# Attention of a hybrid decoder step: probabilities turned two iterations after their scores, with three probability buffers

## What is computed

```python
x = x + 0.5 * swiglu(x, norm_ffn1_g, w_ffn1_in, w_ffn1_out)
q, k, v, qi, ki, wi, lx, lg, qm, gates = mix_inputs(x)        # rmsnorm, h @ w_in, split, q/k norms
o_att = sparse_attention(q, k, v, indexer(qi, wi, ki))        # 8 heads of 64, softmax over the chosen keys
o_lru = rglru_branch(lx, lg)
o_mem = softmax_attention(qm, mk, mv)                         # 4 heads of 128, 256 memory tokens
m = g0 * (o_att @ w_attn_o) + g1 * (o_lru @ w_lru_o) + g2 * (o_mem @ w_mem_o)
x = x + m @ w_out
x = x + 0.5 * swiglu(x, norm_ffn2_g, w_ffn2_in, w_ffn2_out)
```

## Time and profile before

| | |
|---|---|
| median of 3 runs | 3067.04 us (3062.72 to 3069.08) |
| the profiled execution, its own time | 3067.46 us |
| its span | 3065.9 us |
| PE busy, share of the span | 2910.3 us, 95% |
| DVE | 2355.5 us, 77% |
| ACT | 1249.5 us, 41% |
| POOL | 1171.8 us, 38% |
| mean granted TensorE clock | 0.979 of full speed |
| attention stage | about 1653 to 2030 us of the span |

### The profile page before, as it was taken

The page is one execution under the profiler, slowest core; times in us unless marked ns, Lnnn a source line. Parts: engine busy times, 40 slices in busy tenths (PEclk is TensorE's granted clock), DMA queues, the critical chain, the costliest instruction groups (busy, mean ns, idle before and its releaser), DMA issues. The chain is left out here.

```text
span 3065.9 us, 57163 instructions
## 1 busy us (share of the span) xinstructions
PE 2910.3 (95%) x21313; PEld 2739.3 (89%) x21344; DVE 2355.5 (77%) x3879; ACT 1249.5 (41%) x2394; POOL 1171.8 (38%) x823
## 2 busy tenths in 40 slices
PE   6999989999899999999897998989999999899999
PEld 6999989999899999999864666679899999899999
DVE  8888887777749999999943665656568888977776
ACT  5444444434433333234443544531234444443343
POOL 4555545545353331123332000011346555454452
PEclk9999999999999999999988999999999999999999
DMA  4323322232322222312255657534534333223331
GB/s 156 97 90 104 94 80 90 85 96 90 93 74 85 90 88 73 96 43 73 83 193 185 213 192 245 198 121 133 151 89 120 104 94 94 83 86 98 107 97 59
DMA packets 363441, 340.37 MB, mean 111 GB/s; under 512 B 16895, under 2 KB 298082, under 8 KB 363166
## 3 DMA queue, kind: packets, MB, share of 16 engines
q1 hardware_dynamic: 358462, 330.41, 34.8%
q0 software_dynamic: 4128, 4.20, 0.5%
q10 hardware_dynamic: 576, 2.10, 0.2%
HBM read 299.60 MB, written 37.05 MB: 110 GB/s over the span
## 5 line engine op out<-in xcount | busy, mean ns | idle before, releaser
L294 PE MATMUL bank<-op_r_ffn,w_hi 128*128 128x256 f32 (+1 forms) x2992 | 581.0, 292 | 32.3 <-DVE op_r_ffn L275 17.5
L294 PEld LDWEIGHTS bank<-op_r_ffn,w_hi 128*128 128x128 f32 x2992 | 475.9, 191 | 39.1 <-issue 36.4
L294 PE MATMUL bank<-op_r_ffn,w_lo 128*128 128x256 f32 (+1 forms) x1496 | 433.6, 290 | 0.0
L294 PE MATMUL bank<-h_hi,w_hi 128*128 128x362 f32 (+1 forms) x1272 | 421.5, 331 | 6.0 <-ACT qi L2023 2.6
L435 POOL TENSOR_TENSOR w_lo<-sums_ffn,w_hi 128x512 fp32r<-128x512 f32 x214 | 317.7, 1493 | 264.5 <-ACT w_hi L431 264.5
L294 PE MATMUL bank<-h_lo,w_hi 128*128 128x362 f32 (+1 forms) x1272 | 417.9, 329 | 0.0
L294 PE MATMUL bank<-h_hi,w_lo 128*128 128x362 f32 (+1 forms) x1272 | 417.7, 328 | 0.0
L294 PE MATMUL bank<-op_r_ffn,more_hi_ffn 128*128 128x288 f32 (+1 forms) x1936 | 375.6, 292 | 13.8 <-ACT s_ffn L575 5.3
L294 PEld LDWEIGHTS bank<-op_r_ffn,more_hi_ffn 128*128 128x128 f32 x1936 | 306.7, 190 | 17.8 <-issue 8.5
L435 POOL TENSOR_TENSOR more_lo_ffn<-sums_ffn,more_hi_ffn 128x512 fp32r<-128x512 f32 x138 | 203.2, 1479 | 228.5 <-ACT more_hi_ffn L431 228.5
L294 PEld LDWEIGHTS bank<-op_r_ffn,w_lo 128*128 128x128 f32 x1496 | 286.2, 191 | 0.0
(11 more groups left out here) (428 smaller groups left out, 7308.2 us busy)
## 6 DMA issues: line engine op xcount, KB each, us to landing
raw<-in_w_ffn_in SPq DMA_DIRECT2D x132, 512.0 KB, 3.9
raw_ffn<-in_w_ffn_out SPq DMA_DIRECT2D x88, 512.0 KB, 3.6
v_ring<-in_cache_v SPq DMA_DIRECT2D x128, 256.0 KB, 4.6
raw<-in_w_in SPq DMA_DIRECT2D x53, 512.0 KB, 4.9
raw_ffn<-in_w_ffn_in SPq DMA_DIRECT2D x44, 512.0 KB, 3.8
kt_two<-in_cache_k SPq DMA_DIRECT2D x88, 256.0 KB, 3.4
kept_g<-stage SPq DMA_DIRECT2D x24, 544.0 KB, 3.1
gate<-kept_g SPq DMA_DIRECT2D x24, 544.0 KB, 3.6
```

Of the source, the lines that this page charges most:

```text
L294: mm = pe.matmul(out, left, right, start=(start and i == 0 and j == 0), stop=(stop and i == n - 1 and j == 2))
```

## The change

Every step of the pipeline behind the scores is put back by one iteration: PE turns the probabilities of job s - 2 and multiplies those of job s - 3 in iteration s. `oturn`, the loop's end and `merge` follow by one. `pb` has three buffers; the additional 4096 bytes are taken from what `kt_third` had reserved, so that no other address changes. ACT's exp waits for the turn of job s - 3, where it waited for that of job s - 2. No instruction is added or removed in any engine.

```diff
-    for s in range(n + 3):
+    for s in range(n + 4):
         if s < n:
             add("scores", s)
-        if 0 <= s - 3:
-            kind, i, h = jobs[s - 3]
+        if 0 <= s - 4:
+            kind, i, h = jobs[s - 4]
             if kind == "att" and i == 4 and h % 2 == 1:
-                add("oturn", s - 3, 0)
-                add("oturn", s - 3, 1)
+                add("oturn", s - 4, 0)
+                add("oturn", s - 4, 1)
             if kind == "mem" and i % 4 == 3:
-                add("oturn", s - 3, 0)
+                add("oturn", s - 4, 0)
+        if 0 <= s - 3 < n:
+            add("values", s - 3)
+        if s >= n - 1:
+            add("merge", s - n + 1)
         if 0 <= s - 2 < n:
-            add("values", s - 2)
-        if s >= n - 2:
-            add("merge", s - n + 2)
-        if 0 <= s - 1 < n:
-            kind, i, h = jobs[s - 1]
+            kind, i, h = jobs[s - 2]
             blocks = i + 1 if kind == "att" else 2
             for g in range(0, blocks, 4):
-                add("turn", s - 1, g, min(4, blocks - g))
+                add("turn", s - 2, g, min(4, blocks - g))
...
-    kt_third = place("kt_third", [P, GP, 4, P], F32, 12288)
+    kt_third = place("kt_third", [P, GP, 4, P], F32, 8192)
-    pb = place("pb", [P, 2, SEQ], F32, 8192)
+    pb = place("pb", [P, 3, SEQ], F32, 12288)
...
-                    mm = pe.transpose(tb[:, q * P:(q + 1) * P], pb[:, s % 2, (g + q) * P:(g + q + 1) * P],
+                    mm = pe.transpose(tb[:, q * P:(q + 1) * P], pb[:, s % 3, (g + q) * P:(g + q + 1) * P],
...
-                if s >= 2:
-                    act.wait_ge(turned, last_turn(s - 2) + 1)
+                if s >= 3:
+                    act.wait_ge(turned, last_turn(s - 3) + 1)
...
-                act.activation(pb[:, s % 2, 0:keys], bank_t[:, b0:b0 + 2, :].rearrange("p b n -> p (b n)")[:, 0:keys],
+                act.activation(pb[:, s % 3, 0:keys], bank_t[:, b0:b0 + 2, :].rearrange("p b n -> p (b n)")[:, 0:keys],
```

## The result

| | before | changed |
|---|---|---|
| median | 3067.04 us (3061.22 to 3069.08, 5 runs) | 3079.34 us (3078.45 to 3081.26, 5 runs) |
| ratio, 95% interval | | 1.0037 [1.0022, 1.0053] |
| the profiled execution; its span | 3067.46; 3065.9 us | 3081.26; 3079.7 us |
| mean granted clock | 0.979 | 0.975 |

The account below looks back on a forecast made before the run. Transfers bound `mpv` to `sc 3`; from `sc 3` to `mpv`, PE and its helpers do, with ACT's and DVE's chain setting the `pt` groups. 3067.46 + 6.4 - 3.2 + 2.2 + 2.4 = 3075.3 us, own range 3071 to 3081.

Parts of the forecast that it names:

- Odd heads, +1.6 each: Between `sc 3` and `mpv`, `pt 0` waits for ACT's copy behind the long exp; +6.4 us over four heads.
- the prediction's own costs of a block: PE's work in the attention stage: 0.22 us for a values product's block, 0.14 us for a turned block.
- Even heads, -0.8 each: Between `sc 3` and `mpv`, the maximum comes earlier and iteration 7's 1.59 us values wait shrinks; -3.2 us over four heads.
- The clock, +2.4: Odd heads' close waits in iteration 7 lower PE's clock: 0.6 us each, bounds 0 and 2.1; even heads unchanged.
- what the prediction took from the earlier trace: Head 1: 23 instructions, nearly all turns, ran in a row at clock 1.00; so no term for turns slowing PE.
- The end, +2.2: After the last `mpv`: merge moves with the values product, last low parts start at 11.8 us, not 9.6; bounds 0, 4.4.
- the bound of 4.4: Upper bound of the end: 4.4 us if the highs and low parts that swapped places all stay in series.
- From `mpv` to `sc 3`, 0: Transfers end last in this stretch, so PE's gain or loss there goes into the key wait; no change in time.
- (a): Rival: odd heads fall to half clock as head 2 did, 6 us more, end of 4.4: 3083.5 us; chance 0.10.
- (b): Rival: odd heads lose as much as even ones win, only the end is left: 3069.7 us; chance 0.22.
- (c): Rival: faster, PE never waits for `pb` or DVE's copies, three half-clock stretches go too: 3056.6 us; chance 0.12.
- its own point: Where rival (c) decides: whether `pt 0` of odd heads starts before 11.2 us after `sc 3`.

Follow-up runs that it names:

- after_even_banks_keys_early: Changed kernel with the last key group's load issued among the value pages and one extra turn per head (even heads' bank order everywhere): 3041.34 us, ratio 0.9922.
- third_buffer: Kernel before with three probability buffers and no lag changed: 3066.93 us against 3067.74, ratio 0.9996.
- after_keys_early: Changed kernel with the last key group of a sequence issued among the value pages, not behind them: 3055.25 us, ratio 0.9964.
- after_all: Changed kernel with the even heads' banks in every head, the last key group loaded early and the merge at its old place: 3038.01 us, ratio 0.9900.
- before_odd_banks: Kernel before with one small extra turn in iteration 0, so all heads have the bank order of its odd heads: 3063.59 us, ratio 0.9986.
- after_odd_banks: Changed kernel with one small extra turn in iteration 0, so all heads have its odd heads' bank order: 3079.93 us against 3067.19, ratio 1.0037.
- after_merge_old: Changed kernel with the merge put back where the kernel before has it: 3075.82 us against 3069.19, ratio 1.0017.

## Why the prediction was right, and where not

**The direction and the mechanism were right.** The lag was meant to hide exponentials, for which PE waited 1.9 us; what it did was to renumber the turns and to move the merge. The size is less good than it looks: measured up to the last `oturn`, the terms came to 12.2 us in the profiled pair, where 7.8 was forecast. The forecast's own range of 3071 to 3081 isn't the one that its bounds give either: with the end at 0 or 4.4 and the clock at 0 or 2.1 in each odd head they give 3070.7 to 3083.5.

**Odd heads, +1.6 each.** Right: +1.41 at full clock (22.03 to 23.44, 23.6 predicted), by the wait foretold, 1.62 us of `pt 0` for ACT's copy behind the long exp. The values products wait 3.5 us for DVE in four waits, 0.9 each, where 1.0 was forecast. `after_even_banks_keys_early` shows that the banks are the cause: with them changed and the lag left as it is, `pt 0` starts at 11.3 us in place of 12.6 and the odd heads take 22.4. A slip without effect on the sum: by the prediction's own costs of a block (0.22 and 0.14) iterations 5 and 7 get lighter by 0.5 and 0.4 us, not 0.7 and 0.5.

**Even heads, -0.8 each.** Right in kind, -0.53 in size (23.22 to 22.69). The maximum starts 5.18 us after `sc 3` in head 4, as forecast (5.2), and the values product waits 0.22 to 0.3. Together the heads cost +3.5 at full clock where +3.2 was forecast.

**The clock, +2.4.** The size came out at +1.2, and the place was right in two of four odd heads. Above their full-clock times the eight heads stand 12.9 us before (193.9 against 4 x 22.03 + 4 x 23.22) and 14.1 changed (198.6 against 4 x 23.44 + 4 x 22.69). But `third_buffer`, which has the plan of the kernel before, stands only 8.6 above them (189.6), so one pair of executions can't size this term. I had put the half clock behind the two waits of iteration 7. There it was in heads 1 and 5. What I had not foreseen is that it also stood behind `sc 3`, after the key wait, in all four odd heads, and there in heads 2 and 6 as well. The busy view of the changed kernel in head 1 (PEclk is the last number but two), from `sc 3` past `pt 0` (1742.54):

```profile
1728.40:1732.40 4.00, 4.00 (x18) 1.32 (x20) 0.00 (x0) 0.59 (x1) 0.00 (x0) 0.58 0.74 240
1732.40:1736.40 4.00, 4.00 (x42) 3.27 (x41) 3.17 (x6) 1.52 (x4) 0.00 (x0) 1.00 0.82 249
1736.40:1740.40 4.00, 3.29 (x28) 2.28 (x28) 3.84 (x8) 1.97 (x3) 0.00 (x0) 1.00 0.81 240
...
1742.00:1745.40 3.40, 2.86 (x14) 2.79 (x15) 0.42 (x1) 1.74 (x4) 0.00 (x0) 0.50 0.15 61
1745.50:1748.10 2.60, 2.60 (x23) 2.31 (x21) 1.32 (x5) 2.23 (x6) 0.00 (x0) 1.00 0.02 6
```

The first stretch puts `pt 0` at 14.2 us after `sc 3` in all four odd heads, where it is 12.6 at full clock; the second makes it 11.8 us from `pt 0` to `mpv` in heads 1 and 5, where heads 3 and 7, with the clock at 1.00 there, took 10.8. In the second stretch PE ran 14 of the sample's turns and nothing else, and the clock was back at 1.00 behind them: a row of turns alone did not keep it down, in line with what the prediction took from the earlier trace rows.

In the 4 us behind the key wait 18 matmuls ran, most of them at the level of 1.2 GHz; the kernel before had a wait of 1.74 at the same place, and ran 31 there at a clock of 1.00:

```profile
1722.40:1726.40 4.00, 3.99 (x31) 2.59 (x33) 1.19 (x3) 0.70 (x2) 0.00 (x0) 1.00 0.76 261
```

So a wait of the same length is followed by the lower level in one execution and not in the other. In `after_keys_early`, where `sc 3` doesn't wait, three of the four odd heads kept 23.44 us in spite of their waits in iteration 7; head 7 had the stretch at `pt 0` and took 24.65.

**The end, +2.2.** This is the term that was mis-sized, as far as it can be read: the last low parts start 13.4 us after the last `mpv`, not 11.8, +3.8; PE's first branch product comes 3.5 later, and with the longer stretch at half clock behind it the last `oturn` 5.6 later. I had let the highs and low parts overlap with the copies they changed places with; the bound of 4.4, everything in series, was nearer. Putting the merge back recovers the place, with the last low parts at 9.93 us and the first branch product at 10.8 (12.0 and 12.4 in `after_all`); what it gives back in time, 0.0013 to 0.0022, is within or at the edge of the intervals. For the clock at the end the prediction had no term.

**From `mpv` to `sc 3`, 0.** 1.9 us more in the profiled pair, which can't be told from scatter: over the kernels above with late keys the sum lies between 148.0 and 152.7 us. That PE's work there is hidden under the transfers holds; that it isn't free once the cover is gone is shown by the 3.1 us with early keys, which the banks' order makes.

**The rivals.** (a), half clock in iteration 7 of the odd heads, came true in two of four, with about 1.0 us each and not 2.1, and its end of 4.4 was nearer than the forecast's; the time stayed 4 us under it. (b), the heads even out, fell at 23.44 and 22.69, though the sum of an odd and an even head does even out once all heads have the banks of the even ones (`after_all`: 22.42 + 22.69 against 22.03 + 23.22). (c) fell at its own point: `pt 0` of the odd heads starts 12.6 us after `sc 3` at full clock, not before 11.2. In favour of (c) stood the Trainium skill (Perfetto Trace Analysis, Identifying Performance Opportunities), by which a recurring gap can mean too few buffers. The third buffer alone gave 0.9996: the gaps here come from the banks' order and one transfer's place, and the runs bear out none of it for `pb`.

**What stays open.** Why the lower clock follows some waits, at `sc 3` and at `pt 0`, and not others. In `before_odd_banks` seven `sc 3` waited 0.68 to 2.23 us and not one head was slower; head 4 there, the longest wait:

```profile
1858.95 0.40 PE L3208 MATMUL bank<-bias_s,rep 64*32 64x512 bf16 x4 [2.23 <-DMA kt_two<-in_cache_k]
```

The length of the wait doesn't tell the two cases apart, and no run isolates it. How much of the 12.3 us is the clock's is open with it. The scatter of the code ahead of the stage and behind it was seen and not explained.

## What to carry to other kernels

Where several kinds of work share two buffers in alternation, moving one of them one iteration renumbers all the others: write down which engine copies which turn before and after, since that, and not the lag, decided 13 us between the changed kernels with early keys. When a stage has a transfer that closes a loop, look first at what stands ahead of it on its queue: a key load moved past five value pages was worth 25 us, twice what any reordering of the compute was, and it also made most heads repeat to 0.03 us, so that effects of 0.5 us could be read at all. Work that is tied to "the iteration after" another must be told where it should stand when a lag grows, or it moves to the end with it.

## What the runs showed of the hardware that was not expected

- The granted clock stood near half in the 4 us behind key waits of as little as 1.12 us (`after_odd_banks`), and again at `pt 0` of the same heads; they took 2.6 to 3.1 us more (26.02 to 26.51 against 23.44). In the changed kernel two of the four odd heads had both.
- The stage's start moved by 5.1 us between executions of the same code ahead of it, more than most of the terms that were argued about. A single pair of profiled executions can't carry a difference of that size; stretches cut at the same instructions can.
- DVE's last two low parts took 6.31 us in the changed kernel, where POOL makes three low parts of its own beside them, and 3.15 us in `after_merge_old`, where POOL makes one; a single one without POOL takes 1.28.
